# A hybrid-attention encoder layer: attention, out-projection and feed-forward in one block instead of three

## The reference

```python
h = rmsnorm(x, g_norm_mix);  proj = h @ w_in            # q, k, v of both head groups
oa = neighbourhood_attention(qa, ka, va, na_rpb)        # 8 heads, 2-D windows
ob = windowed_gqa_sink(qb, kb, vb, swa_sink)            # 8 heads, |q - k| <= 128
o = concatenate([rmsnorm(oa, g_out_na), rmsnorm(ob, g_out_swa)])
x = x + o @ w_out
h = rmsnorm(x, g_norm_ffn)
x = x + (silu(h @ w_gate) * (h @ w_up)) @ w_down        # width 2816
return rmsnorm(x, g_final)
```

## Time and profile before

| what | us |
|---|---|
| median of 3 runs (lowest, highest) | 2325.01 (2323.56, 2326.05) |
| the profiled execution's own time | 2322.36 |
| its span, first to last instruction | 2320.6 |
| TensorE matmul busy | 2217.7 (96%) |
| VectorE busy | 1441.1 (62%) |
| ScalarE busy | 921.0 (40%) |
| POOL busy | 332.9 (14%) |

### The profile page before, as it was taken

The page is one execution under the profiler, slowest core; times in us unless marked ns, Lnnn a source line. Parts: engine busy times, 40 slices in busy tenths (PEclk is TensorE's granted clock), DMA queues, the critical chain, the costliest instruction groups (busy, mean ns, idle before and its releaser), DMA issues.

```text
span 2320.6 us, 33605 instructions
## 1 busy us (share of the span) xinstructions
PE 2217.7 (96%) x11592; PEld 1830.5 (79%) x11592; DVE 1441.1 (62%) x2761; ACT 921.0 (40%) x1790; POOL 332.9 (14%) x308
## 2 busy tenths in 40 slices
PE   6999999689999989969999999999999999999998
PEld 5888888677877768858888888788888878788886
DVE  5411023289899857768666565856565667666676
ACT  4311122178877733335333333533333333232333
POOL 6301300243334200002021202000000001010100
PEclk9999999899999999989999999999999999999999
DMA  8534333599953145665454546532323276353544
GB/s 243 163 136 132 96 100 96 149 246 242 237 137 108 55 167 195 229 230 210 159 200 161 201 155 243 182 133 78 127 80 125 76 286 239 110 177 109 177 150 153
DMA packets 278072, 376.78 MB, mean 162 GB/s; under 512 B 15578, under 2 KB 184546, under 8 KB 273328
## 3 DMA queue, kind: packets, MB, share of 16 engines
q1 hardware_dynamic: 269920, 354.21, 48.1%
q0 software_dynamic: 5568, 11.87, 2.1%
q10 hardware_dynamic: 2448, 8.91, 1.3%
HBM read 237.84 MB, written 140.31 MB: 163 GB/s over the span
## 4 chain that ended last, share of the span: by engine, by line
PE 51%; DVE 3%; DMA 1%; issue 0%; ACT 0%; DVEq 0%; ACTq 0%
PE ff_psum L1848 12%; PE ff_psum L1850 12%; PE ff_psum L1849 12%; PE ff_psum L1882 5%; PE ff_psum L1884 5%; PE ff_psum L1883 5%; DVE ff_a L1677 1%; DVE ff_x L1775 1%; DMA ff_raw<-in_w_gate 0%; DVE ff_d L1671 0%; DMA ff_d<-down_scratch 0%; DVE ff_ring L1658 0%; DVE ff_h L1663 0%; DVE ff_x L1788 0%; ACT ff_d L1547 0%
## 5 line engine op out<-in xcount | busy, mean ns | idle before, releaser
L1848 PE MATMUL ff_psum<-ff_h,ff_ring 128*128 128x512 f32 x1232 | 480.8, 390 | 14.8 <-DVE ff_ring L1658 12.5
L1849 PE MATMUL ff_psum<-ff_h,ff_ring 128*128 128x512 f32 x1232 | 480.4, 390 | 0.0
L1850 PE MATMUL ff_psum<-ff_h,ff_ring 128*128 128x512 f32 x1232 | 480.3, 390 | 0.0
L1848 PEld LDWEIGHTS ff_psum<-ff_h,ff_ring 128*128 128x128 f32 x1232 | 231.9, 188 | 63.5 <-DVEq L1724 12.9
L1849 PEld LDWEIGHTS ff_psum<-ff_h,ff_ring 128*128 128x128 f32 x1232 | 232.1, 188 | 48.6
L1850 PEld LDWEIGHTS ff_psum<-ff_h,ff_ring 128*128 128x128 f32 x1232 | 232.0, 188 | 48.1
L1882 PE MATMUL ff_psum<-ff_d,ff_a 128*128 128x512 f32 x616 | 240.6, 391 | 8.0 <-DVE ff_x L1775 5.3
L1883 PE MATMUL ff_psum<-ff_d,ff_a 128*128 128x512 f32 x616 | 239.7, 389 | 0.0
L1884 PE MATMUL ff_psum<-ff_d,ff_a 128*128 128x512 f32 x616 | 239.7, 389 | 0.0
L1775 DVE TENSOR_TENSOR ff_x<-ff_psum,ff_x 128x512 f32<-128x512 f32 x224 | 153.8, 689 | 123.5 <-PE ff_psum L1884 123.1
L1658 DVE TENSOR_TENSOR ff_ring<-ff_raw,ff_ring 128x512 fp32r<-128x512 f32 x176 | 130.0, 741 | 107.0 <-ACT ff_ring L1538 107.0
(11 more groups left out here) (149 smaller groups left out, 4100.2 us busy)
## 6 DMA issues: line engine op xcount, KB each, us to landing
acts_scratch<-ff_acts SPq DMA_DIRECT2D x22, 1792.0 KB, 7.9
ff_a<-acts_scratch SPq DMA_DIRECT2D x24, 960.0 KB, 5.0
ff_raw<-in_w_gate SPq DMA_DIRECT2D x42, 512.0 KB, 3.8
ff_raw<-in_w_up SPq DMA_DIRECT2D x42, 512.0 KB, 4.0
att_q_stack<-qk_scratch SPq DMA_DIRECT2D x64, 256.0 KB, 5.1
ff_d<-down_scratch SPq DMA_DIRECT2D x21, 768.0 KB, 6.3
ffn_in_scratch<-mix_h_stage SPq DMA_DIRECT2D x8, 1792.0 KB, 6.2
ff_h<-ffn_in_scratch SPq DMA_DIRECT2D x14, 1024.0 KB, 8.5
```

The lines of the kernel that those rows point to most:

```text
L1848: pe.matmul(out_bank, whi[:, k], hhi[:, :, k], start=(k == 0 and not onto), stop=False, skip_group_check=onto)
L1849: pe.matmul(out_bank, whi[:, k], hlo[:, :, k], start=False, stop=False, skip_group_check=onto)
L1850: last = pe.matmul(out_bank, wlo[:, k], hhi[:, :, k], start=False, stop=(k == 3), skip_group_check=onto)
```

## The change

Projection and its barrier stay. Attention, mix and feed-forward become one block: the barriers and the clearing of semaphores at about 814 and 1038 go, and each engine goes from one phase's instructions to the next one's, held only by semaphores. `mix_phase` and `feed_phase` no longer make blocks but return functions, which the earlier phases call:

- In the last round of attention, SP loads the first two o tiles as soon as the first quarter of the tokens is stored. ScalarE rounds o tile 0 after the copy of unit 28, VectorE makes the rest, and TensorE runs product (0, 0) before the last values.
- Inputs and constants of the mix phase are loaded once the last scores are made; the identity has one place for both phases and isn't loaded again.
- In the mix phase at t = 1 SP loads all of the first weights. They are split at t = 3, 4 and 7 (six tiles), their sums are made at t = 5, 6 and 8. Two parts of h (instead of three) are loaded at t = 10 and 11 and split one tile later.
- The last tile's norm, turning, copy, sums and store now lie among the first products of gate/up: the turning after product 1, the sums after product 1 on VectorE.
- Parts 2 to 4 of h are loaded when TensorE has made the last product of the mix phase; parts 5 and 6 lie where staging buffers were and wait for the last stores. All five are split at step 0 (before: four).
- In the last gate/up step fewer weight parts of the down phase are split early, in other places. All of the memory has a new map.

Core of the diff (the mix and feed functions that only moved out of their blocks are left out):

```diff
+class Memory:
+    W_POOL, MISC, O_TILES = 0, 65536, 187392
+    RAW, SUMS, RING, SPARE = 102400, 118784, 159744, 184320
+    H = (126976, 143360, 0, 16384, O_TILES, 81920, MISC)
...
             for b in range(4):
                 store(ROUNDS - 1, b)
-            for i in range(2):
-                sp.wait_ge(o_stored[i], 16 * (2 * ROUNDS + 1))
+                if b == 0:
+                    mix.load_o(0)
+                    mix.load_o(1)
+                if b == 2:
+                    mix.load_start()
...
-            stream(act, [(TURN_LAG, copy_turned), (0, exp)])
+            stream(act, [(TURN_LAG, copy_turned), (0, exp)], {UNITS + 1: lambda: mix.o_high(0)})
...
+                   {UNITS + NORM_LAG - 1: lambda: mix.o_low(0)})
...
-            stream(pe, [(0, score), (TURN_LAG, turn), (PV_LAG, values)])
+            stream(pe, [(0, score), (TURN_LAG, turn), (PV_LAG, values)],
+                   {UNITS + TURN_LAG - 1: lambda: mix.product(0, 0)})
...
+FIRST_H = (10, 11)
+FIRST_WEIGHTS = {3: (0, 1), 4: (2, 3), 7: (4, 5)}
+FIRST_SUMS = (5, 6)
...
+    def gate_up_sync(mix):
+        mix.products_done(sp)
+        for o in range(EARLY_H, 5):
+            load_h(0, o)
+        load_down(0)
+        mix.store_h(NT - 1)
+        mix.all_stored(sp)
+        for o in (5, 6):
+            load_h(0, o)
...
+    H_SPLITS = {(0, 2 * (o - EARLY_H)): (0, o) for o in range(EARLY_H, SEVEN)}
...
+    def gate_up_vector(mix):
+        mix.norm_dve(NT - 1)
+        w_lo(TURNS - 1)
+        for n in range(WEIGHTS):
...
+            if n + TURNS < WEIGHTS:
+                w_lo(n + TURNS)
...
+            if n == 1:
+                mix.sums(NT - 1)
...
+            if (s, at_step) in H_SPLITS:
+                h_lo(*H_SPLITS[(s, at_step)])
...
+    def tensor(mix):
+        for n in range(WEIGHTS):
+            product(n, mix)
+            if n == 1:
+                mix.turn(NT - 1)
...
-    nc.all_engine_barrier()
-    with nc.cleanup_on_exit():
-        mix_phase(nc, a["x"], w_pool, a["g_ffn"], a["w_gate"], a["w_up"], a["ident"], a["ones"], o_dram, x1_dram,
-                  h_dram, ff)
-    nc.all_engine_barrier()
```

More of the change, by code:

```diff
@@ L19 @@
+from collections import namedtuple
 from contextlib import ExitStack
@@ L618, in body @@
                     step(kind, next_kind, r, s, last=last)
+                    if last and s in then:
+                        then[s]()
             for s in range(deepest):
@@ L1979, in program @@
             ("rel", [P, 2, ROWS_REL * COLS_REL]), ("near_mask", [P, 3, BIAS_COLS]), ("bias", [P, 2, 3, BIAS_COLS]))]
-    ff = FeedMap(nc)
+    mem = Memory(nc)
     with nc.cleanup_on_exit():
```

1669 lines of the change are left out of this document (850 added, 819 removed).

## The result

| | kernel before | changed kernel |
|---|---|---|
| median of 6 runs, us (lowest, highest) | 2325.53 (2323.17, 2329.54) | 2303.02 (2301.31, 2304.72) |
| the profiled execution's own time, us | 2322.36 | 2303.54 |
| its span, us | 2320.6 | 2301.7 |

The ratio of the times is 0.9901, with a 95% interval of 0.9891 to 0.9911: the changed kernel is 22.5 us faster, and 22.4 were forecast. The two profiled executions differ by only 18.8 us: that of before lay 3.2 us under its median, that of after 0.5 us above.

A forecast was written before the change was run, and what follows sets the result against it. TensorE, with matmuls in 96% of the span, was taken as the bound, its idle and slow time lying at two barriers. 7.7 + 14.7 = 22.4 us takes the profiled 2322.36 to 2300.0, median 2302.6; range 2295 to 2312.

The forecast's parts named there:

- First seam, the start of the sums of squares: Attention to mix phase: sums of squares start at 816.9 instead of 826.13, 9.2 us won, 7.7 after the clock loss.
- the branch: VectorE's jump from attention to the mix phase without a barrier: taken as 0.5 us, at most 1.3, at least nothing.
- First seam, the clock: Attention to mix phase: 3.2 us idle before the sums of squares brings half clock on product (0, 1), 1.5 us given back.
- The mix phase: Inside the mix phase: no gain or loss; added splits and sums, at most 2.1 us per tile, fit VectorE's slack.
- Second seam: Mix phase to gate/up: undisturbed start at 1027.3 instead of 1042.0, 14.7 us won, with 3.9 us of waits, no half clock.
- The rest: Down phase, projection and first seven rounds: nothing taken for them.
- the prediction's own sign: Down phase: a length differing by over 1 us would show the prediction wrong.
- Rival 1: Start of gate/up: POOL's work falls whole on the chain of splits, 4.6 us more plus 1.3 for clock: 2308.5; chance 0.13.
- Rival 2: Start of gate/up: transfers of h become the bound, with two slow clocks 10.6 us lost: 2313; chance 0.12.
- Rival 3: Both former barriers: TensorE never waits, best landing times and no half clock, 27.8 us won: 2297; chance 0.13.
- Rival 4: Both former barriers: early loads of o or weights not there in time, waits stay under another name: 2321 to 2325; chance 0.02.
- Rival 5: Mix, gate/up and down: new memory map makes matmuls dearer, at 5 ns each costing 31.6 us: 2334; chance 0.02.

The follow-up runs named there:

- the first seam undone: Changed kernel, but o tiles and constants loaded only once the last results landed, first rounding and product (0, 0) after attention: 2309.77 us, ratio to before 0.9936.
- the second series of runs: The changed kernel timed again without an edit, beside the kernel before: 2304.42 us, ratio to before 0.9919.

## Why the prediction was right

- **First seam, the start of the sums of squares:** forecast 816.9, on the clock of the trace before. Measured 817.76, of which 0.8 us is attention's delay in this execution: within 0.1 us. Two terms that are wrong cancel in it: the branch, taken as 0.5 us, is not visible, and the last copy began at 815.13 instead of about 814.4 on this trace's clock. The constants were there, as argued; with product (0, 0) behind the values they are indeed what comes last.
- **First seam, the clock:** the mis-sized term. I took 1.5 us for the half clock behind the wait. Measured: 12 matmuls at 0.427 instead of 0.2275 us and sums of squares of 0.99 instead of 0.55 us: 2.8 us. With it the seam gives 9.15 - 2.8 = 6.3; the trace shows 6.1 instead of 7.7.
- **The mix phase:** nothing, as forecast. The two waits for turnings are 0.8 and 1.68 us, before 0.6 and 1.70.
- **Second seam:** 14.3 us measured, 14.7 forecast. The forecast waits were 0, 1.8, 1.5, 0 and 0.6 us. They are 0.19, 1.85 and 0.97 at products 4, 6 and 8, none at 10 and 12, and a new one of 0.75 us at step 1. The landing of part 2, POOL's meeting with the splits and their length are as forecast. That no half clock followed these waits was in part luck: behind the wait before product 6, 1.85 and 1.89 us in the changed kernel, the clock stayed up in both of its profiles, but behind the same wait it fell in the traces of the first seam undone (1.89 us) and of product (0, 0) behind the values (1.85 us).
- **What I did not see at the second seam** is that its waits have two causes in series. By the rows the splits beside POOL make the wait before product 6. Taking POOL away gave nothing, since parts 5 and 6 then come too late. Only with the last sums moved as well did the waits go.
- **The rest:** a term put at nothing, and not quite so. The down phase lost 2.3 us in this pair of profiles, which by the prediction's own sign (over 1 us) is wrong. From its first wait of 2.17 us to its last wait of 1.50 us it takes 420.8 us before and 423.1 and 424.2 us in the two profiles of the changed kernel. In the traces of four experiments the clock stays up all the way there, as it does before, and they take 421.6 to 422.5 us. So 0.8 to 1.7 us seem to belong to the change and the rest to the clock. What grew are waits for splits: the longest for `ff_a` is 1.5 to 2.2 us in all traces but one, where others stand in its place, and 1.45 us before. With one profile of before this can't be said more closely, and why these waits grew was not tested.
- **The rule of the skill.** The Trainium skill, page "SBUF — State Buffer", section "Who interferes with whom", says that VectorE and GpSimd share a pair of ports, which is an exclusive lock for a whole instruction. I took a long split as showing only a part of this. The rows agree with the rule to 0.13 us: what is added is what is left of POOL's running instruction. The 3.38 us of the earlier trace rows are that: a split of 2.29 us plus the rest of one. Rival 1 (all of POOL's 7.8 us on the chain) still did not come about: the four sums of tile 15 were over when POOL began, and an instruction waits for the rest of one POOL instruction, not for the group. Two splits of h got 1.1 us longer each and a pair of weight splits 1.6 us, 3.8 us in all. The rival's text says that 3.2 us of this were charged; the sum itself has 2 x 1.09 us for the splits and 3 x 0.6 us for the operations between them, 4.0 us, so the rival was worth 3.8 us more and not 4.6.
- **Rival 2** (transfers become the bound) names the bound that POOL's work hid: the series of store and load shows no wait as long as POOL holds up VectorE before it, and 2 us (products 10 and 12) without POOL. **Rival 3** did not come about. **Rival 4** fell by the timelines. **Rival 5** falls by the pitch: from step 11 to the down phase 422.7 us pass in the changed kernel, and 424.3 before, where the half clock is in it; the new map costs the matmuls nothing.
- **The total** was nearer than its parts. Against the profiles the forecast was too high by 1.6 us (first seam), 0.4 (second seam), 0.8 (attention) and 0.7 (what the half clock gave and took elsewhere), and the profiled execution of before was 3.2 us below its median. That the medians differ by 22.5 us and the forecast said 22.4 is in part luck: the second series of runs gave 20.8.

## What to carry to other kernels

When a barrier goes, list what each engine's queue still holds in front of the first thing that the next phase needs. Twice the remaining wait here was not a long operation but a short one that stood in a queue behind an instruction which itself waited: a sum of squares behind a copy that waited for TensorE, and four sums behind a split that waited for a transfer. Changing the order gave about 5 us at the first, and 3 to 4 us at the second once POOL's group was out of the way. A wait that disappears in an experiment while the time stays shows a second bound in series: look for the next wait further on before giving up the first. And a contended operation is worth moving only if what it then stands beside has slack.

## What the runs showed of the hardware

- **The length of a short wait doesn't decide whether the half clock follows.** One wait in step 11 was 2.25 or 2.26 us long in all 14 profiles of the study. Behind it TensorE kept 2.4 GHz in six of them; in eight the clock fell to 1.2 GHz, in three from the first matmul on and in five some 0.5 to 1.5 us later. From there to the down phase it took 422.7 us in the six and 424.2 to 424.3 us in the eight. Behind the wait of 2.17 us at the start of the down phase, which I had taken as safe, the clock fell in four of 14, in one of the two profiles of the changed kernel and not in the other. It also fell behind one of 1.48 us, and behind both of 3.64 us. What decides it stays open. Each time it costs 1.5 to 2.8 us. Forecasts for a kernel with many waits of 1 to 4 us should carry that as spread.
- **VectorE and POOL lock each other out.** A VectorE addition or subtraction of two tiles in SBUF ends its own time, less 0.13 us, behind the end of POOL's running instruction. POOL's next one waits in turn. The instruction at 1034.39 takes 1.29 us where VectorE leaves it alone, and here 3.23: VectorE's split ends at 1033.08 + 3.38 = 1036.46, and 1.29 - 0.13 us later, at 1037.62, POOL's ends too.
- **The meeting of all engines** with the clearing of semaphores costs about 1.4 us at the first seam: the wait before product (0, 0) is 10.95 us with it and 9.51 us without it.
- **A transfer lands later behind others.** The last store of the sums (1.8 MB) took 6.3 us to land in the changed kernel, 7.5 us when it was issued 8.7 us behind the first of three loads of 1 MB, and 13.4 us when it was issued 7.2 us behind it with a fourth load, of w_down, between them.
